# Output projection of a hybrid decoder block in three rounded products: the splits spread over VectorE, ScalarE and GpSimd, expert loads reordered

## The reference

```python
mod  = silu(c) @ w_ada + b_ada               # six vectors of 1024
h    = rms_norm(x, g_attn) * (1 + sc_a) + sh_a
proj = h @ w_in                              # 512 x 1024 @ 1024 x 3072
a_out = rms_norm(diff_attention(...))        # 4 heads: 512 columns
b_out = rms_norm(stick_breaking(...))        # 8 heads of 64: 512 columns
y = concatenate([a_out, b_out]) @ w_out      # 512 x 1024 @ 1024 x 1024   <- the change
x = x + gt_a * y
h = rms_norm(x, g_ffn) * (1 + sc_f) + sh_f
x = x + gt_f * hier_moe(h)                   # 4 groups x 8 experts of width 256, two chosen per token
```

## Time and profile before

| | |
|---|---|
| median of 3 runs | 646.44 us (645.62 to 649.13) |
| the profiled execution, its own time | 645.13 us |
| its span | 643.0 us |
| TensorE busy | 545.3 us, 85% |
| VectorE busy | 295.3 us, 46% |
| ScalarE busy | 183.3 us, 29% |
| GpSimd busy | 78.6 us, 12% |
| output projection's matmuls (L1631) | 56.2 us |
| DMA, mean over the span | 263 GB/s |

### The profile page before, as it was taken

The page is one execution under the profiler, slowest core; times in us unless marked ns, Lnnn a source line. Parts: engine busy times, 40 slices in busy tenths (PEclk is TensorE's granted clock), DMA queues, the critical chain, the costliest instruction groups (busy, mean ns, idle before and its releaser), DMA issues.

```text
span 643.0 us, 7668 instructions
## 1 busy us (share of the span) xinstructions
PE 545.3 (85%) x2968; PEld 344.8 (54%) x2968; DVE 295.3 (46%) x505; ACT 183.3 (29%) x327; POOL 78.6 (12%) x96
## 2 busy tenths in 40 slices
PE   1399989999888899999999906888999989879796
PEld 1377768677676666665445604444455544434442
DVE  4978680565879536563021285222243222313216
ACT  5255641252453347884133210000000000000002
POOL 8141100000000000000031202111112111110000
PEclk9999999998988998999999956999999999989999
DMA  8986853685153028000841293999999999999966
GB/s 337 395 267 228 318 199 138 209 314 196 58 186 118 2 97 361 1 1 1 361 195 65 113 378 83 391 425 419 420 420 418 419 421 419 420 421 421 401 247 248
DMA packets 42626, 169.28 MB, mean 263 GB/s; under 512 B 7848, under 2 KB 9896, under 8 KB 30308
## 3 DMA queue, kind: packets, MB, share of 16 engines
q1 hardware_dynamic: 32356, 140.81, 54.8%
q0 software_dynamic: 9104, 25.95, 11.4%
q10 hardware_dynamic: 1136, 2.11, 0.8%
HBM read 160.74 MB, written 16.25 MB: 275 GB/s over the span
## 4 chain that ended last, share of the span: by engine, by line
PE 61%; DVE 14%; DMA 12%; SPq 6%; ACT 4%; issue 2%; DVEq 0%; ACTq 0%; POOLq 0%
PE banks L1736 11%; PE banks L1631 9%; PE banks L1756 5%; DMA qkT<-in_w_dram 5%; DMA obuf<-in_w_dram 4%; PE banks L1583 3%; PE banks L1468 3%; PE banks L1470 3%; PE banks L1469 3%; DVE mixT L880 3%; PE banks L1567 2%; PE banks L1460 2%; DMA qkT<-in_w_ada_dram 2%; PE banks L1462 2%; PE banks L1461 2%
## 5 line engine op out<-in xcount | busy, mean ns | idle before, releaser
L1756 PE MATMUL banks<-stage,work 128*64 128x512 f32 x168 | 60.0, 609 | 6.5 <-ACT work L842 5.0
L840 ACT ACTIVATE work<-banks 128x256 f32<-128x256 f32 x16 | 6.1, 383 | 200.7 <-PE banks L1736 200.7
L1736 PE MATMUL banks<-qkT,work 128*64 128x256 f32 x272 | 62.4, 385 | 0.0
L1631 PE MATMUL banks<-stage,mixT 128*128 128x512 f32 x128 | 56.2, 594 | 0.0
L1286 DVE TENSOR_TENSOR work<-banks,gates 128x1024 f32<-128x1024 f32 x15 | 18.4, 1225 | 74.6 <-PE banks L1756 74.6
L1280 DVE TENSOR_TENSOR work<-work,banks 128x256 f32<-128x256 f32 x16 | 6.7, 421 | 87.8 <-ACT work L840 87.8
L1736 PE MATMUL banks<-hT,work 128*64 128x256 f32 x192 | 44.0, 386 | 2.1 <-DMA qkT<-in_w_dram 2.1
L1470 PE MATMUL banks<-hT_hi,w_lo 128*128 128x512 f32 x112 | 44.3, 395 | 0.0
L880 DVE SCALAR_TENSOR_TENSOR mixT<-stage,small,mixT 128x1024 f32<-128x1024 f32 x32 | 41.0, 1283 | 0.7
L1468 PE MATMUL banks<-hT_hi,w_hi 128*128 128x512 f32 x96 | 40.4, 421 | 0.0
L1736 PEld LDWEIGHTS banks<-qkT,work 128*64 128x64 f32 x272 | 36.6, 138 | 5.9 <-issue 0.8
(11 more groups left out here) (293 smaller groups left out, 1153.8 us busy)
## 6 DMA issues: line engine op xcount, KB each, us to landing
stage<-in_w_dram SPq DMA_DIRECT2D x31, 1024.0 KB
qkT<-in_w_dram SPq DMA_DIRECT2D x23, 1024.0 KB
stage<-in_w_ada_dram POOLq DMA_DIRECT2D x16, 1024.0 KB, 5.7
hT<-in_w_dram SPq DMA_DIRECT2D x12, 1024.0 KB
stage<-in_w_in_dram SPq DMA_DIRECT2D x5, 2048.0 KB, 11.4
val<-in_w_dram SPq DMA_DIRECT2D x10, 1024.0 KB
mixT<-in_w_dram SPq DMA_DIRECT2D x10, 1024.0 KB
alibi<-in_w_dram SPq DMA_DIRECT2D x5, 1024.0 KB
```

Of the source, the lines that this page charges most:

```text
L1631: ins = mm(banks[:, w % 5, :], mixT[:, k, t * P:(t + 1) * P], wv[:, k % 4, half * 512:(half + 1) * 512], start=(k == 0), stop=(k == KD - 1))
L1736: ins = mm(banks[half * C:(half + 1) * C, 2, up * F:(up + 1) * F], heT[:, r, k * P + half * C:k * P + (half + 1) * C], ws[2 * place + half ...
L1756: ins = mm(banks[half * C:(half + 1) * C, 4 + 2 * r + col, :], geT[:, fc * P + half * C:fc * P + (half + 1) * C], w2s[2 * place + half][:, ...
```

## The change

The output projection is done in three products as the input projection is. For that mixT and w_out are each split into a rounded part and a rest.

- `mix_hi` takes the first half of qkT, `mix_lo` is written over mixT. For the four heads of the first group ScalarE evacuates twice (`mix_evac`), and VectorE takes the rest two steps after (`mix_rest`, at step fin_step(f) + 3). For the four pairs of the second group VectorE does both (`pair_rest`, in turns 6, 8, 9 and 11).
- `wo_hi` takes `stage[2]` and hT. ScalarE rounds chunks 0 to 3 (`out_round`, steps 12 to 15), GpSimd chunks 4 to 7. VectorE takes the rests (`out_rest`): chunks 0 to 3 in steps 13 to 16, 4 and 5 in turns 2 and 3, 6 in turn 6, and 7 behind the last softplus in turn 8.
- Since hT, half of qkT and `stage[2]` stay in use until the projection ends, SyncE's queue loads five matrices ahead of it and twelve behind it, and one more after the store.

```diff
+OUT_RESTS = {2: 4, 3: 5, 6: 6, 8: 7}
+PAIR_SPLITS = {6: (0,), 8: (1,), 9: (2,), 11: (3,)}
...
+        mix_hi = rounded("mix_hi", [P, KD, T], "qkT")
+        mix_lo = rounded("mix_lo", [P, KD, T], "mixT")
+        wo_hi_parts = (rounded("wo_hi0", [P, 4, D], "stage", 8192), rounded("wo_hi1", [P, 4, D], "hT"))
...
+        def out_chunk(k):
+
+            raw, arrived, value = piece(6 + k // 4)
+            lo = w_lo_parts[:, k // 4, :].rearrange("p (k n) -> p k n", k=4)
+            return raw[:, k % 4, :], wo_hi_parts[k // 4][:, k % 4, :], lo[:, k % 4, :], arrived, value
...
             sp.wait_ge(job_done, job_no[("v", 3, 1)] + 1)
             sp.dma_start(xr[:], x_rows).then_inc(x_again, 16)
-            sp.wait_ge(ada_used, 16)
+            sp.wait_ge(spv_done, SH // 2)
+            load_expert(2, 2)
+            sp.dma_start(slots[1][2], w2_v[1]).then_inc(w2_in[0], 16)
+            sp.dma_start(slots[5][0], w1_v[5]).then_inc(w1_in[2], 16)
+            sp.wait_ge(y_done, 2 * NT)
             load_expert(0, 0)
-            sp.wait_ge(spv_done, SH // 2)
-            load_expert(1, 1)
-            load_expert(2, 2)
-            sp.dma_start(slots[5][0], w1_v[5]).then_inc(w1_in[2], 16)
-            sp.dma_start(slots[5][2], w2_v[5]).then_inc(w2_in[2], 16)
-            sp.wait_ge(y_done, 2 * NT)
+            sp.dma_start(slots[1][0], w1_v[1]).then_inc(w1_in[0], 16)
+            sp.dma_start(slots[1][1], w3_v[1]).then_inc(w3_in[0], 16)
             load_expert(3, 3)
             load_expert(4, 4)
+            sp.dma_start(slots[5][2], w2_v[5]).then_inc(w2_in[2], 16)
             sp.wait_ge(xnb_ready, NT)
             sp.wait_ge(xn_stored, 16 * NT)
...
+            for k in range(4, KD):
+                raw, hi, _, arrived, value = out_chunk(k)
+                pool.wait_ge(arrived, value)
+                pool.wait_ge(job_done, job_no[IN_LAST[5]] + 1)
+                g.tensor_copy(hi, raw).then_inc(wo_hi_pool, 1)
...
             def mix_evac(f):
                 act.wait_ge(T_done, T_no[("fin", f)] + 1)
+                a.activation(mix_hi[:, f, :], banks[:, 6, :], ACT.Copy, scale=out_g[:, 0:1]).then_inc(mix_hi_ready, 1)
                 a.activation(mixT[:, f, :], banks[:, 6, :], ACT.Copy, scale=out_g[:, 0:1]).then_inc(mix_ready, 1)
+
+            def out_round(k):
+                raw, hi, _, arrived, value = out_chunk(k)
+                act.wait_ge(arrived, value)
+                act.wait_ge(ada_used, 16)
+                a.activation(hi, raw, ACT.Copy).then_inc(wo_hi_ready, 1)
...
                 for n in split_at(s):
                     w_round(n)
+                if 12 <= s < 16:
+                    out_round(s - 12)
...
+            def out_rest(k):
+                raw, hi, lo, _, _ = out_chunk(k)
+                if k < 4:
+                    dve.wait_ge(wo_hi_ready, k + 1)
+                else:
+                    dve.wait_ge(wo_hi_pool, k - 3)
+                v.tensor_tensor(lo, raw, hi.bitcast(F32), ALU.subtract).then_inc(wo_split, 1)
+
+            def mix_rest(f):
+                dve.wait_ge(mix_ready, f + 1)
+                v.tensor_tensor(mix_lo[:, f, :], mixT[:, f, :], mix_hi[:, f, :].bitcast(F32),
+                                ALU.subtract).then_inc(mix_split, 1)
...
+            def pair_rest(p):
+
+                dve.wait_ge(pair_mix, p + 1)
+                v.tensor_copy(mix_hi[:, DH + p, :], mixT[:, DH + p, :]).then_inc(pair_hi_ready, 1)
+                dve.wait_ge(pair_hi_ready, p + 1)
+                v.tensor_tensor(mix_lo[:, DH + p, :], mixT[:, DH + p, :], mix_hi[:, DH + p, :].bitcast(F32),
+                                ALU.subtract).then_inc(pair_split, 1)
...
+                if 13 <= s < 17:
+                    out_rest(s - 13)
                 n = s - STICK_0
                 if n % 2 == 1 and 0 <= (n - 5) // 2 < SH // 2:
                     stick_scale((n - 5) // 2)
                 if 0 <= n < SH:
                     softplus(n)
+                for pair in PAIR_SPLITS.get(n, ()):
+                    pair_rest(pair)
+                if n in OUT_RESTS:
+                    out_rest(OUT_RESTS[n])
+                for f in range(DH):
+                    if s == fin_step(f) + 3:
+                        mix_rest(f)
...
                     if w == 0:
-                        for n in (6, 7):
-                            _, arrived, value = piece(n)
-                            pe.wait_ge(arrived, value)
+                        pe.wait_ge(mix_split, DH)
...
-                if ks[-1] >= DH:
-                    pe.wait_ge(pair_mix, ks[-1] - DH + 1)
+                part = slice(half * 512, (half + 1) * 512)
                 for k in ks:
-                    wv = piece(6 + k // 4)[0]
-                    ins = mm(banks[:, w % 5, :], mixT[:, k, t * P:(t + 1) * P],
-                             wv[:, k % 4, half * 512:(half + 1) * 512], start=(k == 0), stop=(k == KD - 1))
+                    _, w_out_hi, w_out_lo, _, _ = out_chunk(k)
+                    if w == 0:
+                        pe.wait_ge(wo_split, k + 1)
+                    if k >= DH and w <= 3:
+                        pe.wait_ge(pair_hi_ready, k - DH + 1)
+                    mm(banks[:, w % 5, :], mix_hi[:, k, t * P:(t + 1) * P], w_out_hi[:, part], start=(k == 0), stop=False)
+                    mm(banks[:, w % 5, :], mix_hi[:, k, t * P:(t + 1) * P], w_out_lo[:, part], start=False, stop=False)
+                    if k >= DH and w <= 3:
+                        pe.wait_ge(pair_split, k - DH + 1)
+                    ins = mm(banks[:, w % 5, :], mix_lo[:, k, t * P:(t + 1) * P], w_out_hi[:, part], start=False,
+                             stop=(k == KD - 1))
```

More of the change, by code:

```diff
@@ L141, in hymba_block @@
         hT = placed_sb("hT", [P, KD, T])
-        qkT = sb("qkT", [P, 16, T])
+        qkT = placed_sb("qkT", [P, 16, T])
         val = sb("val", [P, NT, 1024])
-        mixT = sb("mixT", [P, KD, T])
+        mixT = placed_sb("mixT", [P, KD, T])
         gates = sb("gates", [P, 2, D])
@@ L286, in hymba_block @@
             "z_done", "ln_ready", "soft_ready", "tri_done", "stick_raw", "spv_done"))
+        wo_hi_ready, wo_hi_pool, wo_split = sem("wo_hi_ready"), sem("wo_hi_pool"), sem("wo_split")
+        mix_hi_ready, mix_split, pair_hi_ready, pair_split = (sem(n) for n in (
+            "mix_hi_ready", "mix_split", "pair_hi_ready", "pair_split"))
         pair_sq, pair_sums, pair_rstd, pair_mix = (sem(n) for n in ("pair_sq", "pair_sums", "pair_rstd", "pair_mix"))
```

## The result

The changed kernel is slower: 649.69 us (median of 20 runs, 647.50 to 652.57) beside 645.64 for the kernel before, ratio 1.0057, 95% interval 1.0038 to 1.0076, so about 3.7 us. The ratio is of fast runs alone and is not the quotient of the two medians, which differ by 4.05 us. The forecast was 643.4 with a range to 648.5. The profiled execution has a span of 647.1 us, 4.1 more than before.

What follows compares the result with a forecast made beforehand. The stream of expert weights, started by a serial chain through projection and gather, was taken to set the end. Gain 10.8 - 0.7 - 1.2 - 0.7 - 1.2 = 7.0, gather +4.0: -3.0 us from 646.44, 643.4; range 638.5 to 648.5.

Steps and rivals of the forecast that it cites:

- signs that were to show the forecast wrong: Gather landing in 4 to 5 us, store later than the tables, or GpSimd's and VectorE's delays beyond 4 us.
- TensorE's part of G: Output projection: 192 matmuls in 44.4 us instead of 128 instructions in 55.2, a gain of 10.8 us.
- G: How much earlier the output projection ends, after the added work on VectorE and GpSimd: 7.0 us.
- Step 8: VectorE's mix_rest(0) behind a split of input weights, in a queue TensorE waits for: all counts, 0.7 us.
- Step 13: VectorE's out_rest(0) in front of combine_unit makes TensorE's transposes wait: 1.2 us.
- Turns 4 and 6: mix_rest(3), pair_rest(0) and out_rest(6) delay VectorE's scalings: 0.7 us together, bounds 0.3 and 2.7.
- GpSimd's four copies: Copies of w_out's second half beside softplus(0) and (1) slow VectorE: 1.2 us on the path, bounds 0 and 3.
- The gather: Gather of first rows, behind the projection, takes 8.0 us under load: +4.0 us on the chain, bounds 0 and 5.4.
- The stream loses nothing by the reordering itself: Expert loads behind the projection: 33.7 us at 420 GB/s, places just full by the first release at 36.8 us.
- Rival 1: The gather hardly feels the loads, costing at most 1 us: -6.0 us, 640.4; chance 0.17.
- Rival 2: Insertions in turn 6, step 13 and GpSimd beside VectorE cost more: G 3.2, time 647.2; chance 0.18.
- Rival 3: The last row tile's store, slowed by loads, becomes the gather's wait, 13 us late: +6.0 us, 652.4; chance 0.07.

Runs made afterwards that it cites:

- e4_turns: The changed kernel with VectorE's splits moved, most w_out chunks and the first pair's values to later steps or turns; ratio to the kernel before 0.9982, repeated 0.9997.
- e3_rows_first: The changed kernel with the last five expert loads held until the gathers of the first and second rows landed; ratio to the kernel before 1.0060.
- e8_hold_three: The kernel of e4_turns with GpSimd's four roundings on VectorE and the last three loads held for the first rows; ratio to the kernel before 0.9898, repeated 0.9926.
- e2_copies_only: The kernel before with the four GpSimd copies, results unused, expert 0's loads waiting for them; ratio to the kernel before 1.0085.
- e1_loads_only: The kernel before with only the changed kernel's order of expert loads; ratio to the kernel before 1.0082, some 5.3 us.
- e7_changed_again: The changed kernel once more, unedited; ratio to the kernel before 1.0066.
- e9_copies_late: The kernel of e4_turns with the four GpSimd copies held until VectorE finished the softplus of heads 2, 3 or 5; ratio to the kernel before 0.9967.
- e10_stall_only: The kernel before with three VectorE copies of 128x1024 ahead of head 0's two softplus subtractions, nothing on GpSimd; ratio to the kernel before 1.0122.

## Why the prediction was wrong

The forecast was -3.0 us, and the profiles differ by +4.1. Term by term, what was measured beyond what was predicted: GpSimd's copies +3.2, from the gather to the first release +1.3, the routing +1.6, behind the last load +1.7, D +0.2; against that VectorE's insertions -0.6 and TensorE's own gain -0.4. Two steps failed in their mechanism: what the copies do to TensorE, and what the loads do to the gathers and the stream. The changed kernel also gave one of the signs that were to show the forecast wrong: GpSimd's and VectorE's delays add up to 6.4 us, not under 4.

- *TensorE's part of G*: predicted 10.8, measured 11.2. Right; 0.231 us a matmul from the input projection was the right row.
- *Step 8*: predicted 0.7. TensorE's wait grew from 2.02 to 2.62, but at the next head's transposes it stood at 198.34, against 198.18 before, and at 204.16 against 204.26: 0 in this profile. The granted clock there was not the same, though (0.83 from 190 to 200, before 0.69). From the start of that wait to the later transposes it was 15.3 us before, 15.2 in the changed kernel and 16.1 in its repeat (0.66). So the term lies between 0 and 0.8 and is not told apart from the clock. *Step 13*: predicted 1.2, measured 1.0, shown by e4_turns. *Turns 4 and 6*: predicted 0.7, measured 1.0, of which the moves recover 0.6. In turn 6 `stick_pv(2)` waits 1.92 us for `stick_scale(1)`, as announced, and the ten us behind it are at the full clock:

```profile
298.91 0.61 PE L1659 MATMUL banks<-work,val 128*64 128x512 f32 x1 [1.92 <-DVE mixT L1126]
```
```profile
298.90:308.90 10.00, 9.99 (x56) 7.60 (x56) 7.83 (x12) 3.31 (x6) 0.00 (x0) 1.00 0.01 2
```

- *GpSimd's four copies*: predicted 1.2 with an upper bound of 3, measured 4.4 and 5.2, and 4.5 alone. This is one of the two steps that failed, and its mechanism too. The copies' length was near (1.24 to 1.76 us each, 1.3 predicted), and so was the loss on VectorE (about 2.5 us, 3 predicted). What was missing is what a short gap does to TensorE's clock there: waits of 0.85 and 0.49 us, then some 10 us at 0.50. The prediction had a price for a fall of the clock (bound 2.7), but put it on turn 6, where the longer wait was followed by none. What sets the two places apart is not shown. By the Trainium skill ("SBUF — State Buffer", the port pair that VectorE and GpSimd share) each copy could hold up one VectorE instruction in full. The trace agrees that VectorE is held up (3.23 us for two subtractions where 1.55 was the price, 1.52 where 0.69 was), by about 0.83 us each, less than a copy's length.
- With that, G was 4.8 in the profile, not 7.0, and the projection ended at 358.98, not at 356 to 358.
- *The gather*: predicted +4.0. The first gather landed in 8.3 us, as forecast (8.0). But the step "what the loads do to the gather" stopped at the first; TensorE needs the second one 4 us later, and that took 10.7. Measured from the issue to the release: +5.3 in the changed kernel, +6.0 alone. Of these 4.6 and 5.1 are the later start of the first up product, inside the bound of 5.4 but over the 4.0; 0.7 and 1.0 are that product at the lower clock, for which the prediction had no term.
- *"The stream loses nothing by the reordering itself"*: this sentence failed. 33.7 us of loads and store against 36.8 us until the release was judged to fit, without the gathers' own bytes and their slowing, and as if it were enough that the places are full by then. e3_rows_first shows that loads moved behind the projection push the stream behind them: with the first gather at 3.9 us the end did not move. Only idle time of the DMA engines could be saved, and e8_hold_three saved 3.6 us of its 9.3.
- *The routing*: cost at nothing, measured +1.6, the last logits at the lower clock (3.65 us against 1.99). Likewise 1.7 at the end; since kernels that are the same there show both, this is not put down to the change.
- *Rival 1* (the gather hardly feels the loads, 1 us at most) is refuted: 8.3 and 10.7 us against 4.0. The trace splits the first gather in two. Its first packet moved 1.8 us after the issue before, and 4.3 us after it in the changed kernel (387.49); from there to the landing it took 2.2 us before and 4.0 after. The Trainium skill's rule behind the rival ("DMA: Bandwidth & Descriptors", Queues, rings and completion order) is that each engine goes round the queues packet by packet. The trace agrees for the second part, which is less than twice its old length, but that alone is 1.8 us and not 1 at most. The 2.5 us ahead of the first packet are the larger part, and neither the rival nor the forecast looked at them. From issue to first packet it is 1.8 us again where no loads are in front (e2_copies_only, e3_rows_first), and 3.8 to 4.4 where some are (e1_loads_only, e7_changed_again, e9_copies_late and the three with three loads held). Why is not shown.
- *Rival 2* was nearer on G (3.2; measured 4.8) for partly the right reason: the GpSimd term went beyond its bound of 3, turn 6 stayed well under its 2.7. Its 647.2 lacked the rest of the loads' price and the clock behind the projection. *Rival 3* is refuted: the store landed in 8.6 us.

## What to carry to other kernels

Give a wait of TensorE a second, higher price for the clock that may fall behind it, and look in the profile for which applies: in head 0's softplus waits of 1.3 to 1.8 us cost 4 to 6 us, in turn 6 one of 1.92 was followed by the full clock. Put GpSimd's copies where VectorE idles and not beside its subtractions on the path. When loads are moved behind a point, add up all DMA work from there to the next release, gathers included, since what does not fit moves the end, whichever transfer is served first. Small transfers that are issued together all count if the consumer needs the last of them. If a small transfer on the chain must pass a queue of large ones, hold back as many loads as keep the engines busy until it has landed and no more: three here gave 3 us, five gave none.

## What the runs showed of the hardware

- Three VectorE copies (1.89 us) that made TensorE wait 1.83 us lengthened the stretch by 5.9 us; the granted clock read 0.50 from 250 to 260 (e10_stall_only). A wait of 1.92 us in turn 6 of the changed kernel was followed by ten us at 1.00.
- A GpSimd cast of 128x1024 to the rounded type took 1.04 us where VectorE was idle (e9_copies_late, at 263.62), 1.24 to 1.76 beside its subtractions in the changed kernel, and 1.88 beside one subtraction of 1024 columns (e9_copies_late, at 269.84).
- A gather of 128 rows behind another on GpSimd's queue, beside a full queue of loads, took 10.7 to 11.2 us from issue to landing. The first packet of the first gather moved 1.8 us after the issue with no loads in front and 4.2 to 4.3 beside a full queue of them (changed kernel, its repeat, e1_loads_only, e9_copies_late).
